# Four small moves in a fused two-block kernel: a weight split changes engine, a first product starts on half a tile, one stage's weight splits shift by six units, and the first preparation of causal attention shifts by one round

## The reference

```
# block 1
h = rmsnorm(x) * gain;  proj = h @ w_in                       # 1024 x 3328
q_a, k_a, v_a, g_a, q_b, k_b, v_b, g_b = split(proj)
o_a = full attention (8 heads, 2 key heads, rotary, q/k norm)  * silu(g_a)
o_b = neighbourhood attention (8 heads; 16 rows of 64; windows of 8 rows x 16 columns, bias) * silu(g_b)
x1  = rmsnorm(x + concat(o_a, o_b) @ w_out) * final_gain
# block 2
h = rmsnorm(x1) * gain;  proj = h @ w_in_2                    # 1024 x 4104
y_dn  = gated delta rule (4 heads of 128, chunks of 64: triangular inverse, then a recurrent state)
y_att = causal attention (8 heads of 64) with a bias that adds three dilated patterns
out = x1 + concat(y_dn * silu(z), y_att * silu(gate)) @ w_out_2
```

## Time and profile before

| | us |
|---|---|
| median of 3 runs | 1488.41 |
| lowest, highest of them | 1486.58, 1489.02 |
| the profiled execution, its own time | 1485.48 |
| its span in the profile | 1483.6 |
| TensorE busy in the span | 1438.0 (97%) |
| start, until PE runs without a gap | about 27.8 |
| stage B | about 521 to 636 |
| rounds 8 and 9 of the delta rule | 1227.1 to about 1252 |

### The profile page before, as it was taken

One profiled execution on the slowest core, in us unless ns is written; L12 is line 12 of the kernel. 1 busy time (PEld: TensorE's weight loads), 2 busy tenths in 40 slices (PEclk: granted clock), 3 DMA queues, 4 the chain that ended last, 5 costly groups with the idle time before them and its releaser, 6 DMA issues.

```text
span 1483.6 us, 30802 instructions
## 1 busy us (share of the span) xinstructions
PE 1438.0 (97%) x12682; PEld 1267.8 (85%) x12682; DVE 801.7 (54%) x1474; ACT 619.0 (42%) x1249; POOL 425.0 (29%) x527
## 2 busy tenths in 40 slices
PE   6999999989999999999999999999998998999998
PEld 6999998867777778878899999888897886888887
DVE  5238410149999878735420723452424776888431
ACT  5322121027777677632432113332325554777210
POOL 0212132110000277623202212221205884434320
PEclk9999999999999999999999999999999999999999
DMA  8313222000000043256325244433121021222342
GB/s 261 55 51 104 87 92 70 27 1 1 1 1 1 17 130 105 66 177 171 92 43 59 50 94 85 59 59 56 29 68 41 28 90 44 61 76 71 100 131 82
DMA packets 88017, 105.32 MB, mean 71 GB/s; under 512 B 25343, under 2 KB 72095, under 8 KB 87880
## 3 DMA queue, kind: packets, MB, share of 16 engines
q1 hardware_dynamic: 87880, 103.36, 27.0%
HBM read 80.20 MB, written 23.12 MB: 70 GB/s over the span
## 4 chain that ended last, share of the span: by engine, by line
PE 56%; DVE 4%; ACT 2%; DMA 1%; issue 1%; SPq 0%; POOL 0%; DVEq 0%; ACTq 0%
PE ps L368 22%; PE ps L1336 12%; PE ps L2810 2%; PE ps L1144 2%; PE ps L1128 2%; PE ps L2796 2%; PE ps L2785 1%; PE ps L2215 1%; PE ps L2158 1%; PE ps L2173 1%; DMA p_w_raw<-w_in 1%; PE ps L2773 1%; PE ps L1123 1%; PE ps L1122 1%; PE ps L2786 1%
## 5 line engine op out<-in xcount | busy, mean ns | idle before, releaser
L334 POOL TENSOR_TENSOR p_w_lo<-p_w_raw,p_w_hi 128x2048 fp32r<-128x2048 f32 (+1 forms) x27 | 127.3, 4716 | 506.9 <-ACT p_w_hi L318 506.9
L368 PE MATMUL ps<-p_w_hi,w_out_hi 128*128 128x256 f32 (+1 forms) x640 | 181.9, 284 | 0.4 <-ACT p_spill L393 0.3
L368 PE MATMUL ps<-p_w_hi,w_out_lo 128*128 128x256 f32 (+1 forms) x640 | 179.7, 281 | 0.0
L368 PE MATMUL ps<-p_w_lo,w_out_hi 128*128 128x256 f32 (+1 forms) x640 | 179.6, 281 | 0.0
L368 PE MATMUL ps<-p_w_hi,hT_hi 128*128 128x256 f32 x576 | 163.7, 284 | 1.9 <-DVE hT_lo L140 1.9
L368 PE MATMUL ps<-p_w_hi,hT_lo 128*128 128x256 f32 x576 | 162.7, 282 | 0.0
L368 PE MATMUL ps<-p_w_lo,hT_hi 128*128 128x256 f32 x576 | 162.6, 282 | 0.0
L368 PEld LDWEIGHTS ps<-p_w_hi,w_out_hi 128*128 128x128 f32 x640 | 120.5, 188 | 1.5 <-ACT p_spill L393 0.8
L368 PEld LDWEIGHTS ps<-p_w_lo,w_out_hi 128*128 128x128 f32 x640 | 120.8, 189 | 0.0
L368 PEld LDWEIGHTS ps<-p_w_hi,w_out_lo 128*128 128x128 f32 x640 | 120.6, 188 | 0.0
L368 PEld LDWEIGHTS ps<-p_w_hi,hT_hi 128*128 128x128 f32 x576 | 109.0, 189 | 2.3 <-DVE hT_lo L140 2.3
(11 more groups left out here) (299 smaller groups left out, 3585.0 us busy)
## 6 DMA issues: line engine op xcount, KB each, us to landing
p_w_raw<-w_in SPq DMA_DIRECT2D x26, 1024.0 KB, 8.0
s_gate<-p_spill SPq DMA_DIRECT2D x48, 128.0 KB, 1.8
kbT<-x SPq DMA_DIRECT2D x8, 512.0 KB, 6.9
b_w_raw<-w_out SPq DMA_DIRECT2D x8, 512.0 KB, 6.2
qT<-s_gate SPq DMA_DIRECT2D x8, 512.0 KB, 6.9
qT<-x SPq DMA_DIRECT2D x8, 512.0 KB, 3.5
s_x<-qT SPq DMA_DIRECT2D x8, 512.0 KB, 3.1
c_table<-s_line SPq DMA_DIRECT2D x8, 512.0 KB, 3.6
```

The source lines that it names most:

```text
L334: ops.tensor_tensor(self.w_lo[:, c % 2, :, 0:w], self.raw[:, :, 0:w], self.w_hi[:, c % 2, :, 0:w].bitcast(F32), ALU.subtract).then_inc(sel ...
L368: last = self.nc.tensor.matmul(out, lhs, rhs, start=(kt == 0 and i == 0), stop=(kt == KT - 1 and i == 2))
```

## The change

1. The low part of weight chunk 1 at the start is made by POOL and no more by DVE; `pr.gpsimd` begins with chunk 1.
2. PE begins the first product when the first half of tile 0 has its low part, and no more when both halves have it. Its second half stands behind the transposes of tile 1, which wait for the second half's low part as before.
3. In stage B the casts of `w_out` move from u = 2, 8, ..., 44 to u = 8, 14, ..., 50, and their low parts from u = 4, 10, ..., 46 to u = 10, 16, ..., 52.
4. The four parts of head 0's preparation move from the generator's steps 5 to 8 to its steps 1 to 4, in all four engines' lists. They all use PSUM bank 1 (before: banks 1 to 4), so that part p's transposes wait for the low part of part p-1. The scores of unit 0 go to banks 3 and 4 and stand at step 7, with the waits for `attnT_ready`, `A_ready` and `X0_ready`; the scores of unit 1 come after step 8. PE's first step waits for `khatT_ready` of all tiles and `u_copied` of seven.

```diff
--- before.py
+++ after.py
@@ -405,7 +405,7 @@
 
     def first_tensor(self, pe):
         self.norm.turn(pe, 0)
-        pe.wait_ge(self.norm.lo_ready, 2)
+        pe.wait_ge(self.norm.lo_ready, 1)
         self.multiply(pe, 0, 0, lambda: self.norm.turn(pe, 1))
         for t in range(2, NT + self.LAG + 1):
             if t < NT:
@@ -448,8 +448,6 @@
             if t < NT:
                 self.norm.normalise(dve, t)
             self.norm.split_lo(dve, t - 1)
-            if t == 3:
-                self.split_lo(dve, self.nc.vector, 1)
 
 
 class QueryTurns:
@@ -562,7 +560,7 @@
         pr.sync(sp)
 
     def gpsimd(pool):
-        pr.gpsimd(pool, 2, KEYS_AT + 1)
+        pr.gpsimd(pool, 1, KEYS_AT + 1)
         pool.wait_ge(roped, NT)
         for n in range(2 * A_KV):
             kv, half = n // 2, n % 2
@@ -1217,8 +1215,8 @@
                 store(u - 1)
             if u % ROWS == 4 and u // ROWS + 1 < PAIRS:
                 keys_low(u // ROWS + 1)
-            if u % 6 == 4 and u // 6 < KT:
-                ws.split_lo(dve, nc.vector, u // 6)
+            if u % 6 == 4 and 0 < u // 6 <= KT:
+                ws.split_lo(dve, nc.vector, u // 6 - 1)
             if emptier(u + 1) == "dve":
                 empty(u + 1)
             if u + 4 < n_units:
@@ -1250,8 +1248,8 @@
         for u in range(0, n_units, 2):
             if u % ROWS == 2 and u // ROWS + 1 < PAIRS:
                 keys_high(u // ROWS + 1)
-            if u % 6 == 2 and u // 6 < KT:
-                ws.split_hi(act, nc.scalar.copy, u // 6)
+            if u % 6 == 2 and 0 < u // 6 <= KT:
+                ws.split_hi(act, nc.scalar.copy, u // 6 - 1)
             empty(u)
             if emptier(u + 1) == "act":
                 empty(u + 1)
@@ -2689,11 +2687,11 @@
 
     def score_bank(u):
 
-        return 2 * (u % 2)
+        return 2 * (u % 2) if u else 3
 
     def prep_bank(h, part):
 
-        return part + 1 if h == 0 else PREP_BANK
+        return 1 if h == 0 else PREP_BANK
 
     def emptier(u, piece):
 
@@ -2743,17 +2741,11 @@
             nc.gpsimd.tensor_copy(twice[:, m % 2, :, :, :],
                                   src.unsqueeze(2).to_broadcast([P, 4, 2, HD])).then_inc(doubled, 1)
 
-        double(0, 0)
-        yield
-        double(0, 1)
-        yield
-        for _ in range(3):
+        for part in range(4):
+            double(0, part)
             yield
-        double(0, 2)
-        yield
-        double(0, 3)
-        yield
-        yield
+        for _ in range(4):
+            yield
         pool.wait_ge(delta.s["o_ready"], NT)
         for h in range(ATT_HEADS):
             if h + 1 < ATT_HEADS:
@@ -2766,7 +2758,7 @@
         def turn_prep(h, part):
 
             pe.wait_ge(doubled, 4 * h + part + 1)
-            if h >= 1:
+            if h + part >= 1:
                 pe.wait_ge(low_ready, 4 * h + part)
             for j in range(4):
                 src = twice[:, part % 2, j, :, :].rearrange("p a d -> p (a d)")
@@ -2812,16 +2804,19 @@
                                             v[:, j, h * HD:(h + 1) * HD], start=(j == 0), stop=(j == blocks(u) - 1))
             last.then_inc(out_ready, 1)
 
-        for _ in range(4):
+        pe.wait_ge(delta.s["khatT_ready"], NT)
+        pe.wait_ge(delta.s["u_copied"], NT - 1)
+        for part in range(4):
+            turn_prep(0, part)
             yield
+        yield
+        yield
         pe.wait_ge(delta.s["attnT_ready"], NT)
         pe.wait_ge(delta.s["A_ready"], NT)
         pe.wait_ge(delta.s["X0_ready"], NT)
-        pe.wait_ge(delta.s["u_copied"], NT)
-        for part in range(4):
-            turn_prep(0, part)
-            yield
         scores(0)
+        yield
+        yield
         scores(1)
         for u in range(n_units):
             if u + 2 < n_units:
```

## The result

The changed kernel took 1491.62 us (median of 9 runs, 1490.82 to 1495.26), the kernel before 1487.47 in the same comparison (9 runs, 1486.12 to 1489.02). The ratio is 1.0030, 95% interval 1.0021 to 1.0039: slower by 0.3%, which is 4.15 us between the medians and 4.5 us (3.1 to 5.8) by the ratio. 1491.2 was forecast for the median, and a rise of 2.9 us.

What follows compares the result with a forecast made beforehand. TensorE, busy for 97% of the span, was taken as the bound. Start +1.5, stage B -1.0 and round 8 with round 9 +2.4 gave +2.9 us on 1488.41, named as 1491.2, range 1487.6 to 1493.0.

Steps and rivals of the forecast that it cites:

- POOL's instruction holds DVE's: Start: tile 4's normalisation on DVE waits until POOL's split ends, so tile 4's transposes come 1.6 us later.
- if nothing is held: Start: bound for Edit 1 if DVE runs freely beside POOL, some 0.9 us gained.
- z of level 4: Round 8: starts at 1237.45 where it was 1235.99, +1.46 us, since X waits for low part 1.
- z of level 5: Round 8: starts at 1241.7 where it was 1239.04, +2.66 us, since X waits for part 2's low part.
- the serial chain: Round 8: each part's transposes wait for the previous low part and X stands behind low parts; +3.3 us.
- Part 3 starts 1.05 later: Round 8, after z of level 5: part 3 starts at 1242.75, X waits until 1244.65, +3.4 us.
- Round 8 has the room: Rival: transposes and low parts fall into PE's and DVE's gaps; Edit 4 gives -0.9, total 1488.0 us; chance 0.13.
- POOL does not hold DVE: Rival: the start gains 0.9 to 1.7 us, sum +0.5, total 1488.9 us; chance 0.09.
- The case that ended faster: Round 8 has the room and POOL does not hold DVE together: -2.8 or -3.6, 1485.6 to 1484.8 us; chance 0.07.
- More is lost: Rival: start loses 1.6, an open cast eats stage B's gain, round 9 returns nothing; +5.0, 1493.4 us; chance 0.11.

Runs made afterwards that it cites:

- Edit 1: Kernel before with only change 1, chunk 1's low part on POOL as one instruction: ratio 1.0020 (1.0011 to 1.0029).
- Four pieces: Edit 1 alone, but POOL makes chunk 1's low part as four instructions of a quarter each: ratio 0.9995 (0.9987 to 1.0004) to the kernel before.
- Edit 2: Kernel before with only change 2, the first product waiting for half of tile 0's low part: ratio 1.0001 (0.9992 to 1.0009).
- Edit 3: Kernel before with only change 3, stage B's splits of w_out six units later: ratio 0.9996 (0.9987 to 1.0005).
- Edit 4: Kernel before with only change 4, the preparation in round 8 of the delta rule: ratio 1.0031 (1.0020 to 1.0043).
- the low parts behind X: Edit 4 alone, with DVE's low parts 1 and 2 behind X of levels 3 and 4: ratio 1.0021 (1.0012 to 1.0030) to the kernel before.
- part 3's transposes: Kernel before with Edit 3, Four pieces, and round 9's part 3 transposes right behind part 2's: 1485.84 us against 1489.06, ratio 0.9982.

## Why the prediction was right

**Edit 1.** The theory that POOL's instruction holds DVE's was right, and so was its time: L201 ends 1.08 to 1.09 after POOL (1.14 predicted), the transposes of tile 4 are 1.70 late (1.6 predicted). Four pieces in place of one show it to be the cause. The rule that I had quoted from the Trainium skill, "GPSIMD Engine Reference", section Specifications, has such instructions contend, and these rows agree with it (3.76 us for 1.28). Where I gave 0.9 us gained if nothing is held as the other bound, the pieces gained 0.38 with L201 still held for 0.44, so 0.8 without any hold is my estimate.

**Edit 2.** Counted at -0.1, measured at nothing. The first matmul came 0.6 to 0.9 sooner (0.6 predicted), and the wait for the low part of tile 1 on DVE took it back.

**Edit 3.** -1.0 predicted, -0.98 alone and -0.90 in the changed kernel. What I did not see is that the gap itself varies from 0.55 to 1.68.

**Edit 4.** +2.4 predicted, +2.66 and +2.67 measured at an undisturbed clock. Round 8 cost 3.77 where I had 3.3. z of level 4 came +1.60 after the read (+1.46 predicted), z of level 5 +2.57 (+2.66); the step that was mis-sized is "Part 3 starts 1.05 later": it starts 1.49 after z, since `write`'s own matmuls stand between. Up to z of level 5 the serial chain was even 0.1 too long; this one step, 0.4 short, made the 3.3 too small. Round 9 gave back 1.10 where I had 0.9; the wait of 0.20 ahead of the first row maximum is gone as well, and I had not counted it.

**What was missing from the sum.** The fixed parts add up to 1.70 - 1.0 + 2.66, that is 3.4 us. The measured difference is 4.15 to 4.5, with 3.4 inside its interval. The prediction had no term for the granted clock, and an idle time that grows is not only paid by its length. At the end of the delta rule the clock fell in 4 of 5 profiles of kernels with edit 4, and in 1 of 8 without it, and took 1.2 to 1.5 us where it fell once. Behind the wait for tile 4 it fell in 2 of 3 profiles of kernels with edit 1 in one instruction (waits of 3.30 and 3.60; not with 2.99), and in 1 of 10 of the others, behind a wait of 1.95, and took 1.5 to 2.4. All runs together point the same way. Their mean granted clock is 0.9947 for the changed kernel (9 runs), 0.9946 for edit 1 (11), 0.9950 for edit 4 (7) and 0.9943 with the low parts behind X (12), against 0.9957 and 0.9959 for the kernel before (29 runs each) and 0.9956 to 0.9964 for the five kernels with neither edit 1 in one instruction nor edit 4. As the time of the kernel before goes by some 0.9 us for each 0.001 of this mean (below), I estimate the clock's part in the change at 0.9 us; with the fixed 3.4 that makes 4.3. So edit 1 brings more drops, and so does edit 4 with the low parts behind X; for edit 4 alone seven runs are few. No run set the length of a wait alone, so that the length is the reason is not shown, and when a drop comes stays open.

**Where luck came in.** The median of 1491.2 that I named lies 0.4 us from the measured 1491.62, nearer than the rise does (2.9 for 4.15). It started from the median of three runs before, 1488.41, and nine runs gave 1487.47: a base 0.9 too high made up for most of a rise 1.25 too small. And the single case that I held most likely was a change within 0.2% (0.50 against 0.43 for slower by more), while 0.3% came.

**The rivals.** *Round 8 has the room* fell: its low parts end behind the update's result, and X waits. *POOL does not hold DVE* fell with L201's row. The case that ended faster needed both. *More is lost* came out right in size (+5.0) for some executions, but not by its mechanism: none of stage B's casts lies open (PE is busy for 98.00 of the 98 us from 532 on in the changed kernel), and round 9 gave back 1.10.

## What to carry to other kernels

Before work is moved to an idle engine, look in the trace for two large instructions of both engines that overlap, and see whether one of them is longer than it is alone: here one of 4.57 us on POOL cost 1.70 us and its four quarters gained 0.38, with the same work. In a chain that goes from engine to engine, an inserted piece costs what it puts ahead of each link, on every engine; look for the place where PE waits for something that the inserted work doesn't touch, as with part 3's transposes. And take one execution's profile as a draw: the first profile of before was 2.7 us below a second one, and the four edits together cost some 4.

## What the runs showed of the hardware

- DVE's and POOL's instructions on SBUF tiles held each other in turn. L201 took 3.76 us behind one POOL instruction of 4.57 and 1.72 between pieces of 1.29; the POOL piece behind it took 2.28.
- PE's first matmuls of 256 columns ran 0.21 us apart and later ones 0.12, and the change came anywhere from 13.8 to 17.9 us, while the column of the granted clock read 1.00 in these stretches. The clock's own record in the traces begins only at that moment (15.3 us in the first profile of before, 17.2 in that of the changed kernel), so the column has nothing to read ahead of it. The slower spacing is that of the lower clock: behind tile 4 with edit 1 alone, where the record has 0.50 from 28.5 to 32.0 us, the same matmuls are 0.21 apart. There the spacing of the rows tells the pace and the column doesn't.
- Later drops of the clock are in the column: 0.50, for 3 to 10 us at a time. Over the 29 runs of the kernel before that the single edits were compared with, the time goes with the mean granted clock: 1486.25 us at 0.998 (one run), 1487.2 at 0.997, 1487.9 at 0.996, 1488.9 at 0.995, 1489.8 at 0.994. Much of what varies between its executions goes with the clock.
